# The sample's share of w_b_out moved behind the prompt's w_out in a one-core encoder block

## The reference

```
h = rmsnorm(x, norm1_g); p = h @ w_in            # u, v, c_q, c_kv, k_rope, gate_A, gate_B
a_out = (u * spatial(rmsnorm(v))) @ w_a_out      # "A"
b_out = attention(c_q, c_kv, k_rope) @ w_b_out   # "B": 8 heads, 1024 columns
x = x + (sigmoid(gate_A) * a_out + sigmoid(gate_B) * b_out) @ w_out
t = rmsnorm(x, norm2_g)
aff = softmax(t @ w_router)                      # 16 experts
gates, idx = top_k(aff.T, 2 * n_tok / 16)        # 128 tokens of the prompt, 32 of the sample, per expert
y = x; y[idx] += gates * ((silu(t[idx] @ w_gate) * (t[idx] @ w_up)) @ w_down)
```

## Time and profile before

| | us |
|---|---|
| median of three runs | 2077.86 (2077.16 to 2078.27) |
| the profiled execution | 2075.44 |
| its span in the profile | 2073.7 |
| TensorE busy | 2032.3 |
| VectorE busy | 1348.6 |
| ScalarE busy | 953.6 |
| GpSimd busy | 898.6 |

### The profile page before, as it was taken

The page is one execution under the profiler, slowest core; times in us unless marked ns, Lnnn a source line. Parts: engine busy times, 40 slices in busy tenths (PEclk is TensorE's granted clock), DMA queues, the critical chain, the costliest instruction groups (busy, mean ns, idle before and its releaser), DMA issues.

```text
span 2073.7 us, 33198 instructions
## 1 busy us (share of the span) xinstructions
PE 2032.3 (98%) x13266; PEld 1683.5 (81%) x13266; DVE 1348.6 (65%) x1605; ACT 953.6 (46%) x1180; POOL 898.6 (43%) x632
## 2 busy tenths in 40 slices
PE   8999999999999999999999999899999999999997
PEld 8888888888789889888988887677777777777775
DVE  7864455456767477777754348866777667767774
ACT  8112211113555366666631033455566555555663
POOL 0975555566655376666642601412322222222221
PEclk9999999999999999999999999899999999999999
DMA  4223444333667622232134432688887778888873
GB/s 153 105 104 133 159 162 144 127 92 126 241 231 250 226 64 87 69 115 67 55 112 157 159 143 82 232 352 317 316 303 293 281 284 316 315 315 314 303 285 107
DMA packets 168938, 398.98 MB, mean 192 GB/s; under 512 B 16513, under 2 KB 88193, under 8 KB 168833
## 3 DMA queue, kind: packets, MB, share of 16 engines
q1 hardware_dynamic: 154096, 344.43, 45.3%
q0 software_dynamic: 7680, 20.98, 4.5%
q10 hardware_dynamic: 7056, 32.12, 4.4%
HBM read 318.19 MB, written 79.30 MB: 192 GB/s over the span
## 4 chain that ended last, share of the span: by engine, by line
PE 87%; DVE 7%; POOL 2%; ACT 1%; issue 1%; DMA 1%; SPq 0%; DVEq 0%; ACTq 0%; POOLq 0%
PE PS L1689 25%; PE PS L455 13%; PE PS L456 13%; PE PS L457 13%; PE PS L1720 8%; PE PS L1473 3%; PE PS L1456 1%; PE PS L1460 1%; PE PS L1457 1%; PE PS L1458 1%; PE PS L1459 1%; PE PS L1396 1%; DVE topi L2725 1%; DVE topv L2723 1%; DVE work L2727 1%
## 5 line engine op out<-in xcount | busy, mean ns | idle before, releaser
L455 PE MATMUL PS<-act_hi,w_hi 128*128 128x256 f32 (+1 forms) x800 | 275.3, 344 | 6.5 <-POOL w_lo L930 2.7
L456 PE MATMUL PS<-act_lo,w_hi 128*128 128x256 f32 (+1 forms) x800 | 270.1, 338 | 0.0
L457 PE MATMUL PS<-act_hi,w_lo 128*128 128x256 f32 (+1 forms) x800 | 269.7, 337 | 0.0
L1038 POOL TENSOR_SCALAR prob<-prob,small 128x1024 f32<-128x1024 f32 x64 | 185.7, 2902 | 115.2 <-DVE small L2613 115.2
L1108 POOL DMA_INDIRECT y_s<-ob_s,ixs_s x16 | 44.0, 2751 | 348.6 <-DVE ob_s L2885 348.6
L2830 DVE TENSOR_TENSOR elo<-raw,ehi 128x2048 fp32r<-128x2048 f32 x65 | 148.7, 2290 | 39.2 <-ACT ehi L2215 39.2
L455 PEld LDWEIGHTS PS<-act_hi,w_hi 128*128 128x128 f32 x800 | 151.7, 190 | 24.1 <-POOL w_lo L930 3.0
L457 PEld LDWEIGHTS PS<-act_hi,w_lo 128*128 128x128 f32 x800 | 151.5, 189 | 16.4
L1689 PE MATMUL PS<-ehi,xT_hi 128*128 128x512 f32 x520 | 163.9, 396 | 0.6 <-DVE xT_lo L2798 0.4
L456 PEld LDWEIGHTS PS<-act_lo,w_hi 128*128 128x128 f32 x800 | 151.8, 190 | 14.7 <-issue 0.7
L1689 PE MATMUL PS<-elo,xT_hi 128*128 128x512 f32 x520 | 160.5, 390 | 0.0
(11 more groups left out here) (376 smaller groups left out, 5461.7 us busy)
## 6 DMA issues: line engine op xcount, KB each, us to landing
raw<-in_w_gate SPq DMA_DIRECT2D x64, 1024.0 KB, 8.6
raw_more<-in_w_up SPq DMA_DIRECT2D x32, 1024.0 KB, 12.6
raw_w<-in_w_up SPq DMA_DIRECT2D x32, 1024.0 KB, 15.8
w_raw<-in_w_in SPq DMA_DIRECT2D x16, 1024.0 KB, 7.7
w_raw<-in_w_down SPq DMA_DIRECT2D x15, 1024.0 KB, 6.2
stg<-in_w_down SPq DMA_DIRECT2D x15, 1024.0 KB, 8.6
gt<-in_w_down SPq DMA_DIRECT2D x15, 1024.0 KB, 13.4
raw_end<-in_w_down SPq DMA_DIRECT2D x15, 1024.0 KB, 15.3
```

The costliest lines, as they stand in the source:

```text
L455: pe.matmul(out, lh, rh, start=first, stop=False)
L456: pe.matmul(out, lh, rl, start=False, stop=False)
L457: return pe.matmul(out, ll, rh, start=False, stop=last)
L1038: pool.tensor_scalar(prob[:, n % 3], prob[:, n % 3], prec[:, c:c + 1], None, ALU.mult).then_inc(S["norm_pool"], 1)
```

## The change

Three things are changed together.

- The b tiles are made for the prompt's two blocks alone. ScalarE copies the sample's part of o_hl into the free sample columns of act_hi and act_lo (late_act). The w_b_out tiles are loaded once more, each into the columns of a prompt chunk whose w_out is done (load_late_w), and split there by GpSimd (split_late). After the prompt's last half chunk of w_out TensorE makes the sample's eight tiles (late_tile). ScalarE copies each out of PSUM (late_copy) and rounds z (late_high); GpSimd multiplies, adds (z_late) and subtracts (z_late_low). SP loads the sample's parts of gate B and of A tile by tile (load_late_z). The turn of the first half's chosen tokens and the flip come in late tiles 4 and 5. Then follow the sample's two chunks of w_out, and after them the turn of the second half's chosen tokens. The 48 transposes of the identity are gone.
- The first two pieces of expert 0 are loaded after the late tiles, and rounded by ScalarE and subtracted by GpSimd ahead of the sample's chunks (expert_high, first_low). GpSimd also subtracts pieces 3 and 5 (POOL_LOW).
- In expert 0's frame the sample's lists are turned behind product 0, its selection is made behind piece 4, its chosen tokens are turned behind product 4, its rows behind product 5, and its first few_product stands behind product 6 (before: behind product 4). The norms of chunks 8 and 9 moved from GpSimd to VectorE.

```diff
-            for i in range(2, KD - 1):
-                for b in range(3):
+                for b in range(2):
...
+            def load_late_z(i):
+                if i > 1:
+                    sp.wait_ge(S["part_lo"], at("part_lo", 3 * KD + i - 1))
+                _, gate, za = late_in(i)
+                sp.dma_start(gate, g_d[KD + i][:, TP:T]).then_inc(gt_in[i % 2], 16)
+                sp.dma_start(za, za_d[i][:, TP:T]).then_inc(ld_in[i % 2], 16)
...
             for c in range(NCH):
-                if c == NCH - 1:
+                if c == NCH_P - 1:
+                    load_late_w(c)
+                    for i in range(2, KD):
+                        load_late_z(i)
+                    sp.wait_ge(S["tile_pe"], late_no(KD - 1))
+                    for kk in range(2):
+                        read_piece("g", 0, kk, kk)
+                if c == NCH - 2:
                     sp.wait_ge(S["out_pe"], 2 * NCH)
-                    for kk in range(4):
+                    for kk in range(2, 4):
                         read_piece("g", 0, kk, kk)
...
+            def z_late(i):
+                o, gate, za = late_in(i)
+                pool.wait_ge(S["evac"], late_no(i))
+                pool.wait_ge(gt_in[i % 2], 16 * (KD + i // 2 + 1))
+                pool.wait_ge(ld_in[i % 2], 16 * (KD + i // 2 + 1))
+                pool.tensor_tensor(gate, o, gate, ALU.mult).then_inc(S["pool_step"], 1)
+                pool.wait_ge(S["pool_step"], H + i + 1)
+                pool.tensor_tensor(za, gate, za, ALU.add).then_inc(S["z_sum"], 1)
...
+            for i in range(KD - 1):
+                split_late(i)
+            for i in range(KD):
+                z_late(i)
+                if i > 0:
+                    z_late_low(i - 1)
+                if i == 1:
+                    split_late(KD - 1)
+            z_late_low(KD - 1)
...
+            def late_tile(i):
+                hi, lo = late_w(i)
+                pe.wait_ge(S["w_split"], split_no(G_END + i))
...
+                for k in range(KD):
+                    last = mm3(pe, late_bank(i), hi[:, k], lo[:, k], act_hi[:, k, TP:T], act_lo[:, k, TP:T], k == 0, k == KD - 1)
...
+            for i in range(KD):
+                late_tile(i)
+            pe.wait_ge(S["evac"], late_no(KD - 1))
+            for c in range(NCH_P, NCH):
+                half_chunk(c, 0, c - 1 if c > NCH_P else None)
+                half_chunk(c, 1, None)
+            pe.wait_ge(S["x2_act"], 3)
+            turn_chosen(1)
...
-            keep_going(20)
-            turn_chosen(1, 4)
-            keep_going(14)
-            turn_lists(2)
-            keep_going(14)
...
                     if is0 and l == 0:
-                        turn_chosen(2, 5)
-                    if is0 and l == 3:
+                        turn_lists(2)
+                    if is0 and l == 4:
+                        turn_chosen(2)
+                    if is0 and l == 5:
                         turn_xs(0)
...
-                    if l == 4 and is0:
+                    if l == 6 and is0:
                         pe.wait_ge(S["xs_dve"], 1)
                         few_product(6, lambda k: quarters(xT_s, k), 0)
```

More of the change, by code:

```diff
@@ L57 @@
 G_A, G_B, G_OUT = 2, 10, 18
+G_END = G_OUT + 8
 PAIRS = 18
@@ L388, in build @@
             raw = sb(s, "raw", [P, 4, 2, D])
-            ehi = sb(s, "ehi", [P, 3, 2, D], F32R)
-            elo = sb(s, "elo", [P, 3, 2, D], F32R)
+            ehi = [sb(s, f"ehi{n}", [P, 2, D], F32R) for n in (2, 0, 1)]
+            ehi = [ehi[1], ehi[2], ehi[0]]
+            elo = [sb(s, f"elo{n}", [P, 2, D], F32R) for n in range(3)]
         raws = [raw[:, n] for n in range(4)] + [raw_more[:, n] for n in range(2)] + [raw_w2[:, n] for n in range(2)]
@@ L1626, in _, with half_chunk @@
                     out_product(c, 0, k)
-            pe.wait_ge(S["evac"], 3 * G_OUT)
+            pe.wait_ge(S["evac"], tile_no(G_OUT))
             pe.wait_ge(S["r_in"], 50 + STRIPS)
-            halves = [(c, 1) for c in range(HC)] + [(c, h) for c in range(HC, NCH) for h in range(2)]
-            for i, (c, h) in enumerate(halves):
+            def half_chunk(c, h, ready):
                 if c >= HC:
                     pe.wait_ge(S["x2_dve"], out_no(c, h) - 4)
-                ready = halves[i - 1][0] if i > 0 and halves[i - 1][1] else None
                 for k in range(KD):
@@ new lines, in _ @@
+            for c in range(HC):
+                half_chunk(c, 1, c - 1 if c else None)
+            for c in range(HC, NCH_P):
+                half_chunk(c, 0, c - 1)
+                half_chunk(c, 1, None)
+            pe.wait_ge(S["late_act"], 2)
+            for i in range(KD):
[3 more added lines that the diff above has]
+                half_chunk(c, 0, c - 1 if c > NCH_P else None)
+                half_chunk(c, 1, None)
@@ L1650, in _ @@
+            pe.wait_ge(S["x2_act"], 3)
+            turn_chosen(1)
             channels(NCH - 1)
             strip_products(NCH - 1)
-            logits(NCH - 1)
-            turn_chosen(0, 2)
-            pe.wait_ge(S["chosen_act"], 1)
-            pe.matmul(bank(3)[:, 0:2 * E], flip[:], chosen[:].rearrange("p v e -> p (v e)"), start=True,
-                      stop=True).then_inc(S["chosen_pe"], 1)
-            def keep_going(n):
-                for _ in range(n):
-                    pe.transpose(bank(6)[:, 0:P], ident[:], ident[:])
@@ L1663, in _ @@
-            keep_going(20)
-            turn_chosen(1, 4)
-            keep_going(14)
-            turn_lists(2)
-            keep_going(14)
+            for n in range(NCH_P, NCH):
+                logits(n)
             def turn_x(e):
@@ L2192, in list_copy, with root_again @@
                 n = GROUPS[grp][1] * P
-                act.activation(dst[:], PS[0:E, (0, 1, 2)[grp] * BANK:(0, 1, 2)[grp] * BANK + n], ACT.Copy).then_inc(S["affT_act"], 1)
-            for n in range(NCH):
+                act.activation(dst[:], list_bank(grp)[:, 0:n], ACT.Copy).then_inc(S["affT_act"], 1)
+            def root_again(n):
+                act.activation(std2[:, n + 1:n + 2], ssq2[:, n:n + 1], ACT.Sqrt, bias=epsc,
+                               scale=1.0 / D).then_inc(S["ssq_act"], 1)
+            for n in range(NCH_P):
+                second_root(n)
+                channels(n)
+                if n == NCH_P - 1:
+                    late_copy(0)
+                strip_copy(n)
+                if n == NCH_P - 1:
+                    late_copy(1)
+                    late_high(0)
+                if n in (HC - 1, NCH_P - 1):
+                    powers(n // HC)
+                    root_again(n)
+                    list_copy(n // HC)
+            for i in range(2, KD):
+                late_copy(i)
+                late_high(i - 1)
+                if i == 4:
+                    act.wait_ge(S["chosen_pe"], 1)
+                    act.activation(chosen[:].rearrange("p v e -> p (v e)"), chosen_bank(0), ACT.Copy)\
+                        .then_inc(S["chosen_act"], 1)
+                if i == 5:
+                    act.wait_ge(S["chosen_pe"], 2)
+                    act.activation(turned[:].rearrange("p v e -> p (v e)"), flipped_bank(), ACT.Copy)\
+                        .then_inc(S["chosen_act"], 1)
+            late_high(KD - 1)
+            for n in range(NCH_P, NCH):
+                if n == NCH_P:
+                    expert_high(0, 0)
+                    expert_high(1, 1)
+                for h in range(2):
+                    sample_sum(n, h)
                 second_root(n)
```

280 lines of the change are left out of this document (175 added, 105 removed).

## The result

The changed kernel took 2099.03 us in the median of four runs (2093.78 to 2099.71), the kernel before 2078.07 (2077.16 to 2081.80). The ratio is 1.0096 with a 95% interval of 1.0084 to 1.0107: 21 us slower, where 11 were forecast. The direction was right; the time lies outside the range that was given.

The account below looks back on a forecast made before the run. TensorE, busy 98% of the span, was taken as the bound, so time falls only where it waits or runs slowly. 0.6 + 5.6 + 1.0 + 3.9 = 11.1 us later, 2089 against the median of 2077.9; range 2080 to 2096.

Parts of the forecast that it names:

- Step 1: Sample's w_b tiles leave their old place: 23.0 us moved, 0.7 lost, prompt's w_out ends 22.3 us earlier.
- Step 2: Eight late tiles: exposed loads make the z_late period 5.0 us against TensorE's 2.88; sample's w_out ends 14.3 us later.
- Step 3: From the sample's w_out to the gathered rows: 0.7 us more for two expert pieces issued at the same moment.
- From the rows to the third product: Expert 0's start: 9.9 us from gathered rows to third product, where it was 8.8; that product 0.6 us later.
- Steps 4 and 5: Expert 0 and expert 1's weights: waits of 5.6 us, 1.0 for contention and 3.9 for late xT_lo.
- rival D: Heavier: full GpSimd and VectorE exclusion, 3 us load pairs, low clock behind two expert waits; 18.5 us later, 2096, chance 0.14.
- The contention: VectorE's piece 4 beside GpSimd's subtractions in expert 0: 0 to 2.3 us slower, 1.0 taken.
- The base: Profiled execution before the change took 2075.4 us, 2.4 under the median of 2077.9 that the forecast was set against.
- A: Late tiles: the z_late chain keeps TensorE's pace, period 3.1 us or less; 1.4 us faster, 2076.5, chance 0.08.
- B: Expert 0 and expert 1's weights cost nothing, their waits being covered; 0.6 us later, 2078.5, chance 0.07.
- C: A and B at once, over late tiles and experts: 11.9 us faster, 2066, chance 0.03.
- E: Lighter: z_late period 4.3 us, no low clock after the k = 6 wait, no contention; 4 later, 2082, chance 0.10.

Follow-up runs that it names:

- e3: Changed kernel with pieces 2 and 3 of expert 0 loaded only when the first gathered rows have landed; 2099.88 us, 1.0112 of the kernel before.
- e1: The changed kernel run once more, nothing edited; 2096.22 us, 1.0094 of the kernel before.
- e2: Changed kernel with gate B and A share of each late tile loaded two tiles ahead into free low_raw columns; 2085.65 us, 1.0045 of before.

## Why the prediction was wrong, step by step

The mechanisms stood where the forecast put them; four sizes did not. The times are those of the profile after, with the 5.0 us taken off that were lost ahead of the change; the forecast is in brackets.

- **Step 1, the work taken away: held.** The first late tile starts at 1252.29, that is 23.0 us less than before [22.3 less].
- **Step 2, the late tiles: right in kind, 2.2 us short.** The sample's w_out ends at 1322.47, 16.5 later than before [14.3]. TensorE's waits were 1.10, 2.77, 1.44, 2.12 and 3.83 us; the forecast had 2, 2.5, 2 and 4. GpSimd ends the last of them, so its chain decides. It is z_late of tile 2, five periods, and z_late of tile 7:

```profile
1269.47 0.74 POOL L1215 TENSOR_TENSOR gt<-xr,gt 128x256 f32<-128x256 f32 x1 [1.95 <-ACT xr L2290]
...
1295.34 0.72 POOL L1215 TENSOR_TENSOR gt<-xr,gt 128x256 f32<-128x256 f32 x1 [2.77 <-DMA stg<-za_d]
```

The chain starts at 1264.5 [1262.4], 2.1 late. GpSimd was done with its split at 1262.5, as forecast, but then waited 1.95 us for the copy of tile 2: TensorE had waited 2.77 us for the lists [about 2] and then made this tile in part at the lower clock, which was charged at nothing here. The period was 5.17 [5.0], with the pair of loads 2.6 to 3.5 from issue to use [2.5]; five of them add 0.9. So TensorE is released at 1292.6 [1289.8], and from there to the end it took 24.9 us [25.4]. The windows of the lower clock:

```profile
1266.00:1270.00 4.00, 4.00 (x27) 4.00 (x26) 2.91 (x7) 1.27 (x3) 2.06 (x2) 0.72 0.04 13
...
1290.00:1292.00 2.00, 2.00 (x6) 1.51 (x6) 1.93 (x5) 0.09 (x1) 1.58 (x3) 0.50 0.00 0
...
1300.00:1302.00 2.00, 2.00 (x6) 1.58 (x5) 1.90 (x6) 1.38 (x2) 1.92 (x2) 0.50 0.15 61
```

With the windows beside them (0.71 from 1264, 0.68 from 1288, 0.74 from 1298, 0.90 from 1302) TensorE lost some 1.5 us behind the wait for the lists, 1.6 around 1290 and 1.7 behind the last wait [1.8]. The 1.6 in the middle cost nothing: GpSimd ended the wait behind them, which they only shortened.

- **Step 3, the gather: 3.5 us short, the largest miss behind the start of the change, and the step that failed.** "Two pieces of expert weights (2 MB) are now issued at the same moment; bounds 0 and 1.5, I take 0.7." From the end of w_out to the rows it took 11.3 us [7.8]. The gather and what SP issued around it:

```profile
1324.40 1.80 POOL L1159 DMA_INDIRECT xs_p<-h_d,ixg_p  x1 [11.77 <-DVE ixg_p L2959]
```

```profile
1322.49 0.90 SPq L920 DMA_DIRECT2D raw<-in_w_gate  x2
1325.18 0.34 SPq L936 DMA_DIRECT2D h_d<-w_raw  x1
1325.56 0.43 SPq L939 DMA_DIRECT2D y_s<-xr  x1
1326.57 0.32 SPq L936 DMA_DIRECT2D h_d<-w_raw  x1
1326.93 0.58 SPq L939 DMA_DIRECT2D y_s<-xr  x1
```

Its rows could be used 9.35 us after issue, 4.8 before, 7.05 in e3 without the pieces: 4.6 us more where 0.7 were charged. The upper bound of 1.5 had no row behind it, and the four stores were left out: the norms had moved to VectorE behind the turn, and their stores with them. Between the gather's issue and its landing the 16 DMA engines were busy throughout:

```profile
1324.50:1333.70 9.20, 1.36 (x20) 0.97 (x20) 2.01 (x3) 1.29 (x3) 1.70 (x1) 0.78 1.01 374
```

At 374 GB/s that is 3.4 MB, of which half a megabyte was the gather's. The view of the DMA queues (packets, MB, share; q1 is SP's queue, q0 the gather's), first from the issue to 1330.3 us, then from there to 1333.2:

```profile
q1 hardware_dynamic: 525, 2.04, 98.5%
...
q1 hardware_dynamic: 183, 0.66, 55.6%
q0 software_dynamic: 143, 0.52, 45.3%
```

For 5.9 us no packet of the gather moved, while SP's queue moved 2.04 MB, about the size of the two pieces; before, its first packet came 1.9 us after issue. Moving it then took 2.9 us, 2.5 before. The Trainium skill ("DMA: Bandwidth & Descriptors", section "Queues, rings and completion order") says that each DMA engine alternates between the queues that have work, a packet at a time. The second stretch agrees, with 143 packets against 183; the first doesn't show it, and that is where the time went. Why the gather's packets start so late was not settled.

- **From the rows to the third product: held.** 9.7 us [9.9].
- **Steps 4 and 5, the experts: 2.8 us short.** From the third product to the fourth of expert 1's frame it took 13.3 us more than before [10.5]. The waits themselves were 1.39, 2.49, 2.40 and 3.14, in sum 9.4 [10.6]. Behind the second and the third the clock fell again, which stood in rival D alone:

```profile
1356.00:1360.00 4.00, 3.95 (x12) 3.16 (x13) 2.93 (x4) 1.90 (x2) 2.31 (x1) 0.63 0.00 0
...
1364.00:1368.00 4.00, 4.00 (x15) 2.81 (x16) 2.35 (x2) 0.00 (x0) 2.59 (x3) 0.59 0.05 9
```

That is 1.5 and 1.6 us. The first only shortened the wait for the sample's rows, which the gather ended; the second delayed the sample's product, and with it expert 1's loads. The contention was under-sized: VectorE's piece 4 took 4.25 us beside GpSimd's piece 3, 2.0 more than alone [1.0], and GpSimd's copy of the sample's row numbers, ahead of their gather, took 2.31 us beside VectorE's piece 6, where it takes 0.18 alone [nothing].

```profile
1345.65 4.25 DVE L3002 TENSOR_TENSOR elo<-raw_more,ehi 128x2048 fp32r<-128x2048 f32 x1 [2.32 <-ACT ehi L2398]
```

```profile
1357.22 2.31 POOL L1166 COPY ixg_s<-rows 128x1 uint32<-128x1 uint32 x1 [2.85 <-DVE gates L2991]
```

Along this path, counted from the third product: the turn of the sample's tokens came 12.6 us behind it [11.3], the rows 7.2 later [6.6, with a gather of 4.1 that took 2.9], the end of the sample's product 8.3 later [6.5], and expert 1's fourth product 20.5 behind that [21.3]. The rule of the Trainium skill that the forecast weighed would have paid 2.3 for piece 4, and came nearer than the middle that was taken.
- **The base: 5.0 us.** The forecast was made against one profile that had none of the accidents ahead of 1050 us. Against medians this term is mostly gone: 19.7 us in e1 for 11.1 forecast.

The sum: 2.2 + 3.5 - 0.2 + 2.8 + 5.0 = 13.3 on top of 11.1 gives the 24.4 of the two profiles. Without the base it gives 19.4, against 19.7 for e1's median. Rival D had the right direction and two of the causes, but gave the gather nothing. The rivals A, B and C were refuted in the changed kernel; e2 shows A's mechanism at work once the loads are free of the chain: its period is TensorE's. One sum of the rivals doesn't close: E takes back 1.7 us for contention where 1.0 was charged, so it stands for 5 us later, not 4.

The experiments cut the loss in another way, by what takes it away: exposed loads 10.6 us, expert order 12.2. The slow gather is in neither as a separate cost: taken away with either order it gave 1.8 and 0.4 us, so it must be seen as one of several things that were late together.

## What to carry to other kernels

A double buffer does not hide a load when the step that frees the buffer and the step that needs it stand next to each other on one engine; release it by an earlier event (here TensorE's), or put it in memory that this event frees. Look for low clock behind each wait of 2 us and more, and charge it only where no later wait, ended by another engine or a load, takes it up. When steps move, list the loads and stores that move with them; here a small gather came as late as if it had to let the 2 MB issued ahead of it go first.

## What the runs showed of the hardware

- An indirect gather of 128 rows (0.5 MB) could be used 4.5 and 4.8 us after issue alone, 7.05 beside 2 MB of stores, and 9.2 to 10.2 with 2 MB of loads issued ahead of it and 2 MB of stores behind, in eight profiles. Its first packet moved 1.9 us after issue alone, 4.9 beside the stores and 5.7 to 6.0 in the eight.
- A VectorE step of 0.19 us took 2.59 when it started during a GpSimd subtraction, and ended with it. The Trainium skill ("SBUF — State Buffer", section "Who interferes with whom") says that VectorE's instructions with two inputs in SBUF need the port that it shares with GpSimd, and that this port is held for a whole instruction while the other engine stops. The trace agrees with both numbers, 2.59 and 4.25 us. The other way round, GpSimd's copy of 0.18 us took 2.31 when it started beside VectorE's subtraction of 2.29, and ended with it.
- The clock: in the profile after, five of TensorE's six waits between 2.12 and 3.83 us from the late tiles on were followed, within 2 us of work, by a stretch at 0.50, the 1.2 GHz level. The sixth, of 3.14 us, was not (1.00 from 1382 to 1386), nor was the one of 2.77 us in e1 (1.00 from 1262 to 1266), so such a wait doesn't always bring it. In 10 of 16 profiles it was also under 1.00 between 508 and 516 us, with TensorE busy throughout; what brings that on was not settled.
